# Two MLPs of a small transformer pair: one 512-column matmul for both fp32 parts of the tokens

## What is computed

```
# block 1, its MLP: up 1024 -> 4096, down 4096 -> 1024
h = rms_norm(x, pre_mlp_norm)
m = square(relu(h @ w_up)) @ w_down
x = x + rms_norm(m, post_mlp_norm)

# block 2, its MLP: gate and up 1024 -> 2816, down 2816 -> 1024
h2 = rmsnorm(x, g_ffn)
x = x + (silu(h2 @ w_ff_gate) * (h2 @ w_ff_up)) @ w_ff_down
return rmsnorm(x, g_final)
```

## Time and profile before

| | us |
|---|---|
| three timed executions, median | 974.71 (974.29 to 975.01) |
| the profiled execution, its own time | 973.31 |
| its span, first to last instruction | 971.4 |
| TensorE busy | 934.6, 96% of the span |
| DVE busy | 568.7, 59% |
| ACT busy | 453.3, 47% |
| TensorE's granted clock, mean | 0.994 of full speed |

### The profile page before, as it was taken

The page is one execution under the profiler, slowest core; times in us unless marked ns, Lnnn a source line. Parts: engine busy times, 40 slices in busy tenths (PEclk is TensorE's granted clock), DMA queues, the critical chain, the costliest instruction groups (busy, mean ns, idle before and its releaser), DMA issues.

```text
span 971.4 us, 13913 instructions
## 1 busy us (share of the span) xinstructions
PE 934.6 (96%) x6068; PEld 842.1 (87%) x6068; DVE 568.7 (59%) x629; ACT 453.3 (47%) x527; POOL 92.0 (9%) x93
## 2 busy tenths in 40 slices
PE   6998879999999999999999999999999999999997
PEld 5997659887999999889998988888888799999996
DVE  5679784376555554667684546455456555354453
ACT  5865345547444433555544232632535454343432
POOL 2006321000000000010030330101100000000000
PEclk9999999999999999999999999999999999999999
DMA  8551420042644455454465434444435544555431
GB/s 315 205 195 65 157 95 26 23 153 92 245 183 173 173 187 205 172 204 165 173 218 185 169 133 175 174 173 173 168 147 192 188 152 180 210 174 215 164 142 43
DMA packets 24221, 159.87 MB, mean 165 GB/s; under 512 B 3241, under 2 KB 3513, under 8 KB 5857
## 3 DMA queue, kind: packets, MB, share of 16 engines
q1 hardware_dynamic: 21600, 152.58, 42.7%
q0 software_dynamic: 2272, 6.24, 1.8%
q10 hardware_dynamic: 288, 0.17, 0.1%
HBM read 157.91 MB, written 2.63 MB: 165 GB/s over the span
## 4 chain that ended last, share of the span: by engine, by line
PE 85%; DVE 8%; ACT 4%; issue 1%; POOL 0%; DMA 0%; DVEq 0%; POOLq 0%; ACTq 0%
PE bank L402 39%; PE bank L431 31%; PE bank L456 4%; PE bank L381 2%; DVE t_wl L1346 2%; PE bank L876 1%; PE bank L674 1%; DVE t_cout L1362 1%; PE bank L514 1%; PE bank L697 1%; ACT t_wh L944 1%; DVE t_gs L1358 1%; ACT t_hold L952 1%; PE bank L827 1%; DVE t_kb L1354 1%
## 5 line engine op out<-in xcount | busy, mean ns | idle before, releaser
L1346 DVE TENSOR_TENSOR t_wl<-t_raw,t_wh 128x2048 fp32r<-128x2048 f32 (+1 forms) x144 | 328.1, 2302 | 179.0 <-ACT t_wh L944 177.9
L402 PE MATMUL bank<-t_hh,t_wh 128*128 128x256 f32 x1192 | 339.6, 285 | 1.6 <-DVE t_hl L1362 1.2
L402 PE MATMUL bank<-t_hl,t_wh 128*128 128x256 f32 x1192 | 338.1, 284 | 0.0
L402 PE MATMUL bank<-t_hh,t_wl 128*128 128x256 f32 x1192 | 338.1, 284 | 0.0
L944 ACT CAST t_wh<-t_raw 128x2048 fp32r<-128x2048 f32 (+1 forms) x144 | 268.9, 1899 | 35.8 <-PE bank L402 20.0
L402 PEld LDWEIGHTS bank<-t_hh,t_wh 128*128 128x128 f32 x1192 | 229.5, 193 | 4.5 <-DVE t_hl L1362 2.7
L402 PEld LDWEIGHTS bank<-t_hl,t_wh 128*128 128x128 f32 x1192 | 229.6, 193 | 1.2
L402 PEld LDWEIGHTS bank<-t_hh,t_wl 128*128 128x128 f32 x1192 | 229.5, 193 | 0.0
L431 PE MATMUL bank<-t_wh,t_hh 128*128 128x512 f32 x160 | 63.8, 407 | 0.0
L431 PE MATMUL bank<-t_wh,t_hl 128*128 128x512 f32 x160 | 61.7, 394 | 0.0
L431 PE MATMUL bank<-t_wl,t_hh 128*128 128x512 f32 x160 | 61.6, 393 | 0.0
(11 more groups left out here) (292 smaller groups left out, 1228.6 us busy)
## 6 DMA issues: line engine op xcount, KB each, us to landing
t_raw<-in_W SPq DMA_DIRECT2D x143, 1024.0 KB, 4.9
skew<-scr POOLq DMA_DIRECT2D x1, 1536.0 KB, 17.4
t_x<-in_x SPq DMA_DIRECT2D x2, 512.0 KB, 4.2
t_T<-skew POOLq DMA_DIRECT2D x8, 128.0 KB, 2.4
out<-t_xt SPq DMA_DIRECT2D x4, 256.0 KB, 2.1
t_tab<-in_tab POOLq DMA_DIRECT2D x1, 640.0 KB, 6.4
t_raw<-in_W SPq DMA_DIRECT2D x1, 512.0 KB, 6.5
t_T<-skew POOLq DMA_DIRECT2D x8, 64.0 KB, 2.3
```

The lines of the kernel that those rows point to most:

```text
L402: m = e.matmul(bank[b][:, c * S:c * S + S], W[w][:, h, k * 128 * nt + c * 128:k * 128 * nt + c * 128 + 128], H[a][:, k, :], start=first, s ...
L1346: e.tensor_tensor(M.wl[:, h, 0:n], M.raw[:, r, 0:n], M.wh[:, h, 0:n].bitcast(F32), ALU.subtract).then_inc(q.sem, q.tick(("lo", i)))
```

## The change

- The eight PSUM banks become one tensor `banks`, and `t_hh` and `t_hl` become one tensor `t_hx` in which hi and lo of a k-slice lie side by side, 512 adjoining columns.
- A new `wide_unit` takes the place of `b_unit` for f2 to f15 and for all fg and fu: 14 + 22 = 36 units. It holds two adjoining banks, one for each feature tile. For each k-slice: `t_wh` of tile 0 and of tile 1, each times 512 columns (hi and lo at once, landing in the left and the right half of the bank), then `t_wl` of both tiles times 256 columns (hi), into the left half. That is 32 matmuls, 16 of 512 and 16 of 256 columns, k-slices outermost. It starts at an even bank, so it may skip one.
- The product is now the sum of the two halves of a bank. ACT copies the right halves of both banks (`tail`, `gtail`, `utail`), and DVE adds the left halves to that (`t_rl`, `t_gsum`, `t_usum`).
- First MLP: Relu and Square on ACT are gone. DVE makes the sum, then `max(x, 0) * x` in one instruction (`t_sqb`), ACT rounds that to `t_mh`, DVE subtracts. For tiles 0 and 1, which are transposed and not split, DVE copies the bank to `t_rl`.
- Second MLP: Silu reads `t_gsum`; the product on DVE reads `t_usum`.
- Everything ahead of the first MLP and between the two is computed as before.

```diff
+def both(banks, b, part):
+    return banks[:, b:b + 2, part * S:part * S + S]
...
-    M.bank = [top.enter_context(nc.psum_tensor(f"bank{i}", [128, 512], F32)) for i in range(8)]
+    M.banks = top.enter_context(nc.psum_tensor("banks", [128, 8, 512], F32))
+    M.bank = [M.banks[:, i, :] for i in range(8)]
-    M.hh = sb(top, "hh", [128, 8, S], FR)
-    M.hl = sb(top, "hl", [128, 8, S], FR)
+    M.hx = sb(top, "hx", [128, 8, 2, S], FR)
+    M.hh, M.hl = M.hx[:, :, 0, :], M.hx[:, :, 1, :]
...
+            def wide_unit(tile, arrived, by, name, mid=None):
+                turn[0] += turn[0] % 2
+                b, i = take(tile), next_unit()
+                take((tile, 1))
...
+                q.wait_ge(DV, ("lo", i))
+                opened(b)
+                opened(b + 1)
+                for k in range(8):
+                    arrived(k)
+                    for w in range(2):
+                        for c in range(2):
+                            wk = slice(k * 256 + c * 128, k * 256 + c * 128 + 128)
+                            if w == 0:
+                                e.matmul(bank[b + c], M.wh[:, h, wk], M.hx[:, k, :, :].rearrange("p a s -> p (a s)"),
+                                         start=k == 0, stop=False)
+                            else:
+                                m = e.matmul(bank[b + c][:, 0:S], M.wl[:, h, wk], M.hh[:, k, :], start=False,
+                                             stop=k == 7)
...
             for i in range(2, 16):
-                b_unit(("f", i), x_mlp, AC, ("rl", i), mid=turn_up if i == 2 else None)
+                wide_unit(("f", i), x_mlp, DV, ("fs", i), mid=turn_up if i == 2 else None)
...
-                b_unit(("fg", i), x_ffn, AC, ("gl", i), k_outer=i == 0)
-                b_unit(("fu", i), x_ffn, DV, ("gu", i))
+                wide_unit(("fg", i), x_ffn, DV, ("gsum", i))
+                wide_unit(("fu", i), x_ffn, DV, ("usum", i))
...
# ACT, first MLP
-            def relu(i):
+            def tail(i):
+                q_ = i % 2
+                q.wait_ge(PE, ("f", i))
+                if i >= 4:
+                    q.wait_ge(DV, ("fs", i - 2))
+                e.copy(halves(M.tail[:, q_, :]), both(M.banks, at["f", i], 1)).then_inc(q.sem, q.tick(("tail", i)))
+            def leading(i):
                 q_, r = i % 2, i % 3
...
+                q.wait_ge(DV, ("sqb", i))
...
+                e.copy(M.mh[:, 2 * r:2 * r + 2, :].rearrange("p a s -> p (a s)"), M.sqb[:, q_, :]).then_inc(
...
                 if i == 2:
-                    relu(0)
-                    relu(1)
-                relu(i)
+                    leading(0)
+                    leading(1)
+                tail(i)
+                leading(i)
...
# ACT, second MLP
-                e.activation(M.gl[:, q_, :], bank[at["fg", i]][:], ACT.Silu).then_inc(q.sem, q.tick(("gl", i)))
+                e.copy(halves(M.gtail[:, q_, :]), both(M.banks, at["fg", i], 1)).then_inc(q.sem, q.tick(("gtail", i)))
+                q.wait_ge(DV, ("gsum", i))
+                e.activation(M.gl[:, q_, :], M.gsum[:, q_, :], ACT.Silu).then_inc(q.sem, q.tick(("gl", i)))
                 next_unit()
+                q.wait_ge(PE, ("fu", i))
+                e.copy(halves(M.utail[:, q_, :]), both(M.banks, at["fu", i], 1)).then_inc(q.sem, q.tick(("utail", i)))
                 q.wait_ge(DV, ("gu", i))
...
# DVE, first MLP
             def square(i):
...
-                q.wait_ge(AC, ("rl", i))
-                tt(M.sqb[:, q_, :], M.rl[:, q_, :], M.rl[:, q_, :], ALU.mult, ("sqb", i))
+                q.wait_ge(PE, ("f", i))
+                if i < 2:
+                    e.tensor_copy(M.rl[:, q_, :], bank[at["f", i]]).then_inc(q.sem, q.tick(("fs", i)))
+                else:
+                    q.wait_ge(AC, ("tail", i))
+                    tt(rl, both(M.banks, at["f", i], 0), halves(M.tail[:, q_, :]), ALU.add, ("fs", i))
...
+                stt(M.sqb[:, q_, :], M.rl[:, q_, :], 0.0, M.rl[:, q_, :], ALU.max, ALU.mult, ("sqb", i))
                 q.wait_ge(q, ("sqb", i))
                 q.wait_ge(AC, ("mh", i))
...
# DVE, second MLP
                 next_unit()
-                next_unit()
-                q.wait_ge(PE, ("fu", i))
+                q.wait_ge(AC, ("gtail", i))
+                tt(halves(M.gsum[:, s, :]), both(M.banks, at["fg", i], 0), halves(M.gtail[:, s, :]), ALU.add,
+                   ("gsum", i))
+                next_unit()
+                q.wait_ge(AC, ("utail", i))
+                tt(halves(M.usum[:, s, :]), both(M.banks, at["fu", i], 0), halves(M.utail[:, s, :]), ALU.add,
+                   ("usum", i))
+                q.wait_ge(q, ("usum", i))
                 q.wait_ge(AC, ("gl", i))
-                tt(M.gl[:, s, :], M.gl[:, s, :], bank[at["fu", i]][:], ALU.mult, ("gu", i))
+                tt(M.gl[:, s, :], M.gl[:, s, :], M.usum[:, s, :], ALU.mult, ("gu", i))
```

More of the change, by code:

```diff
@@ L293, in memory @@
         M.up = sb(p2, "up", [128, 2, 512])
+        M.tail = sb(p2, "tail", [128, 2, 512])
         M.rl = sb(p2, "rl", [128, 2, 512])
@@ L325, in memory @@
         M.gl = sb(p4, "gl", [128, 2, 512])
+        M.gsum = sb(p4, "gsum", [128, 2, 512])
+        M.usum = sb(p4, "usum", [128, 2, 512])
+        M.gtail = sb(p4, "gtail", [128, 2, 512])
+        M.utail = sb(p4, "utail", [128, 2, 512])
         M.fh = sb(p4, "fh", [128, 4, S], FR)
@@ L409, in b_unit @@
                 drain(b, by, name)
+            def wide_unit(tile, arrived, by, name, mid=None):
+                turn[0] += turn[0] % 2
+                b, i = take(tile), next_unit()
+                take((tile, 1))
+                assert PLAN[i][0] == "B" and b % 2 == 0, (i, PLAN[i], tile)
+                h = i % HR
+                q.wait_ge(DV, ("lo", i))
[12 more added lines that the diff above has]
+                                             stop=k == 7)
+                    if k == 7:
+                        m.then_inc(q.sem, q.tick(tile, ("unit", i)))
+                    if mid and k == 3:
+                        mid()
+                drain(b, by, name)
+                drain(b + 1, by, name)
             def a_unit(kind, name, act, arrived, ks, outs, first, last, hooks={}):
@@ L1175, in scalar @@
             between("mlp", par("pre_mlp"), lambda t: ("up", t), M.up)
-            def relu(i):
-                q_, r = i % 2, i % 3
-                q.wait_ge(PE, ("f", i))
-                if i >= 2:
-                    q.wait_ge(DV, ("ml", i - 2))
-                e.activation(M.rl[:, q_, :], bank[at["f", i]][:], ACT.Relu).then_inc(q.sem, q.tick(("rl", i)))
-                q.wait_ge(q, ("rl", i))
+            def tail(i):
[5 more added lines that the diff above has]
+            def leading(i):
+                q_, r = i % 2, i % 3
+                q.wait_ge(DV, ("sqb", i))
                 if i >= 3:
                     q.wait_ge(PE, (("down", i - 3), 1))
-                e.activation(M.mh[:, 2 * r:2 * r + 2, :].rearrange("p a s -> p (a s)"), M.rl[:, q_, :],
-                             ACT.Square).then_inc(q.sem, q.tick(("mh", i)))
+                e.copy(M.mh[:, 2 * r:2 * r + 2, :].rearrange("p a s -> p (a s)"), M.sqb[:, q_, :]).then_inc(
+                    q.sem, q.tick(("mh", i)))
             for i in range(2, 16):
```

6 lines of the change are left out of this document (5 added, 1 removed).

## The result

| | kernel before | changed kernel |
|---|---|---|
| median of 20 timed executions each, us | 974.56 (972.66 to 977.30) | 972.72 (971.25 to 973.95) |
| ratio | | 0.9982, 95% interval 0.9974 to 0.9990 |
| profiled execution, its own time | 973.31 | 973.27 |
| its span | 971.4 | 971.5 |

The change saves 1.84 us, 0.2% (1.0 to 2.5 us by the interval), where 4.4 were forecast. It is faster, and 2.6 us of the gain are missing.

What follows compares the result with a forecast made beforehand. TensorE, busy 96% of the span, was taken to bound the kernel. Matmuls -7.5 us and stalls +1.4, +0.8 and +0.9 us sum to -4.4 us, from 974.71 to 970.3 us (chance 0.72), range 968.4 to 974.4.

Steps and rivals of the forecast that it cites:

- What bounds the kernel, and the matmuls: Both MLPs: TensorE bounds; 576 pairs of narrow matmuls become wide ones, each saving 0.013 us, -7.5 us in all.
- rivals 1 to 3: Matmuls save less: width changes not given back (972.3, 0.07); half fixed part stays (974.3, 0.06); wide costs two narrow (977.8, 0.04).
- The 2.5 ns a matmul of the Trainium skill: Wide units' matmuls: by the skill's rule a pair saves only 2.5 ns, 1.4 us in all; 976.4 us, chance 0.01.
- The three stalls: New TensorE waits at the first MLP's start and the second's start and end: +1.4, +0.8 and +0.9 us.
- Down 0: First down unit of the first MLP: waits for `t_ml` of tile 0 behind a now serial chain, +1.4 us.
- fg0: First gate unit of the second MLP: its wide form waits for `t_hl` of k-slice 3, not 1, +0.8 us.
- the closing pair: End of the second MLP: waits for `t_fl` of tile 10 behind ACT's copy and DVE's sum, +0.9 us.
- Nothing more is late: First MLP after down 0: work queued behind the waiting DVE and ACT instructions still comes in time, no further cost.
- Rival 4: DVE, from the sum to the next `t_wl`: conversions late in 25 rounds; +10 us at 0.4 us each, 980, chance 0.05.
- a clock below 1.00: TensorE's granted clock behind the new stalls: listed only among the signs that the forecast is wrong, with no size.
- the rival nearest to it, 1: Eight changes up in width in each wide unit are not given back: price 2.0 us, 972.3 us, chance 0.07.

Runs made afterwards that it cites:

- e1: Changed kernel with the second MLP taken back to narrow units, only the first MLP wide; 975.17 us, ratio 1.0003 against the kernel before.

## Why the prediction was wrong, point by point

**What bounds the kernel, and the matmuls: right.** 7.2 us for 7.5. A pair saves 0.207 / 16 = 0.0129 us in the first MLP and 0.197 / 16 = 0.0123 in the second; rivals 1 to 3 are out. The 2.5 ns a matmul of the Trainium skill ("TensorE: Matmul & The Clock Gate", section "Wait — 56ns, not 53.3ns?"), 1.4 us as an estimate, is out with them: the rounds fell by five times that.

**The three stalls: right in place and cause, each a little small.** Down 0 1.5 for 1.4, fg0 0.9 for 0.8, the closing pair 1.1 for 0.9: together 3.5 for 3.1. DVE's durations were met within 0.06 us (`t_sqb` 0.69 for 0.75); what was missing is time between instructions, such as the 0.15 us from the end of DVE's `t_ml` to TensorE (246.62 to 246.77).

**"Nothing more is late": the step that failed in the small.** Some 0.3 us went at the end of the first MLP: the transposes start 0.63 us behind the last matmul's start where it was 0.37. The last round's longer way (1.5 us was counted) pushes the three conversions, and DVE's first read of the result waits for them. DVE's timeline before, then after:

```profile
393.36 6.70 DVE L1346 TENSOR_TENSOR t_wl<-t_raw,t_wh 128x2048 fp32r<-128x2048 f32 x3 [1.12 <-ACT t_wh L944]
400.46 0.69 DVE L1354 TENSOR_TENSOR t_xt<-bank,t_hold 128x512 f32<-128x512 f32 x1 [0.41 <-ACT t_hold L952]
```

```profile
394.89 6.70 DVE L1395 TENSOR_TENSOR t_wl<-t_raw,t_wh 128x2048 fp32r<-128x2048 f32 x3 [1.12 <-ACT t_wh L984]
401.51 0.68 DVE L1403 TENSOR_TENSOR t_xt<-banks,t_hold 128x512 f32<-128x512 f32 x1
```

Before, 0.41 us passed between them, waiting for ACT; now DVE goes straight on, late. The prediction checked what those conversions are needed for in a round, and not who else stands behind the last of them. Rival 4 in its main sense didn't happen: no wait of TensorE on `t_wl` was added.

**The sum: the step that failed is the clock, a term put at nothing.** The misses above are 0.3 + 0.4 + 0.3 = 1.0 us of the 2.6 that are missing. The other 1.6 is, as far as the runs show, the granted clock: 2.1 us each time that it falls there, in three traces of three against one of five. The prediction took 1.00 in the earlier trace rows as a property of the stretch, and named a clock below 1.00 only as a sign of error, with no rival, price or chance. The trace of before could have priced it: its opening has three half-clock stretches of 3.4 us, which are most of why its mean clock is 0.994, and an engine that is busy all through one would lose half of it, 1.7 us, as an estimate. The four units at the start of the second MLP stand behind two idle stretches, one of which the change makes longer. And the place that it named, behind the new stalls, is not the whole of it: the clock fell at 777.0, ahead of fg0's wait (777.45 to 779.37), and in e1 without the longer wait.

**The range held the time**, and the rival nearest to it, 1 at 972.3, is wrong in its mechanism. That its number is near is an accident: the time of an execution can't tell 2 us of narrow steps from 2 us at half clock; the table by stretches does, since one lies in every unit and the other in four.

## What to carry to other kernels

Price the clock where TensorE stands behind idle time: a mean of 1.00 in one trace does not make the stretch safe, since one trace in five of the same kernel read otherwise and paid 2 us, and a change that only shifts the stretch in time can turn the one case into the other. When a change saves a hundredth of a microsecond many times and lengthens a few handovers, mend the handovers in the same edit: here that took the change from -1.8 to -5.5 us (-7.2 to -3.1). And of each delayed instruction ask for every reader behind it on its engine, at the end of the loop too, where the reader is another one.
